# Score matmuls of two heads issued back to back in the neighbourhood attentions

## What is computed

```python
q = a @ w_q * 64 ** -0.5                     # 8 heads of 64, 256 rows
k, v = [ctx; a] @ w_k, [ctx; a] @ w_v        # 512 keys: 256 local, 256 context
s_loc = q k_loc^T + bias(rpb, window)        # -1e30 outside the window of 16 columns
s_ctx = q k_ctx^T
p = softmax([s_loc, s_ctx]);  y = p @ v
```

## Time and profile before

| | us |
|---|---|
| median of 3 runs (lowest, highest) | 3045.1 (3044.39, 3056.07) |
| the profiled execution: its time | 3047.46 |
| the profiled execution: its span | 3045.7 |
| PE busy in the span | 2736.5 (90%), 13754 matmul records |
| DVE busy | 788.7 (26%) |
| ACT busy | 453.7 (15%) |
| mean granted TensorE clock | 0.952 |
| "na0", from its first weight load to that of the low projection behind it | 1820.16 to 1864.61 |
| "na1", first weight load | 2482.05 |

### The profile page before, as it was taken

The page is one execution under the profiler, slowest core; times in us unless marked ns, Lnnn a source line. Parts: engine busy times, 40 slices in busy tenths (PEclk is TensorE's granted clock), DMA queues, the critical chain, the costliest instruction groups (busy, mean ns, idle before and its releaser), DMA issues.

```text
span 3045.7 us, 33992 instructions
## 1 busy us (share of the span) xinstructions
PE 2736.5 (90%) x13754; PEld 1856.9 (61%) x13754; DVE 788.7 (26%) x1893; ACT 453.7 (15%) x971; POOL 74.8 (2%) x144
## 2 busy tenths in 40 slices
PE   6998987889989969899999598898999897998998
PEld 2554544446567845555554356587788544687886
DVE  1344202221121261111111414414642224313002
ACT  2132002121120021000000113301000122301000
POOL 0000000000000000000000000000000000000000
PEclk9998998899999979999999799999999999999999
DMA  9874998999966519999999432143675211133330
GB/s 397 330 328 185 372 413 350 383 421 410 422 279 262 197 64 400 422 411 422 419 422 422 165 120 77 56 148 129 258 283 205 111 55 56 74 148 135 142 138 14
DMA packets 117580, 764.86 MB, mean 251 GB/s; under 512 B 12784, under 2 KB 15600, under 8 KB 34224
## 3 DMA queue, kind: packets, MB, share of 16 engines
q1 hardware_dynamic: 94352, 680.57, 55.3%
q0 software_dynamic: 20224, 74.26, 6.2%
q10 hardware_dynamic: 2848, 7.83, 0.6%
HBM read 759.20 MB, written 3.41 MB: 250 GB/s over the span
## 4 chain that ended last, share of the span: by engine, by line
PE 75%; DMA 14%; DVE 6%; issue 2%; ACT 2%; SPq 1%; POOL 0%; ACTq 0%; DVEq 0%
PE bank L542 73%; DMA ring<-in_stream 13%; PE bank L841 1%; PE bank L830 1%; SPq L422 1%; DMA work<-in_stream 1%; PE bank L546 1%; DVE work L1835 1%; DVE MX L1897 0%; ACT work L1432 0%; DVE work L1914 0%; DVE work L1694 0%; DVE work L1687 0%; DVE work L2349 0%; DVE X L2114 0%
## 5 line engine op out<-in xcount | busy, mean ns | idle before, releaser
L542 PE MATMUL bank<-A,ring 128*128 128x256 f32 (+1 forms) x3088 | 712.0, 390 | 17.7 <-issue 7.7
L542 PEld LDWEIGHTS bank<-A,ring 128*128 128x128 f32 x3088 | 588.8, 191 | 134.8 <-issue 43.7
L542 PE MATMUL bank<-ring,A 128*32 128x512 f32 (+3 forms) x2304 | 418.4, 638 | 82.3 <-DMA ring<-in_stream 71.4
L542 PE MATMUL bank<-work,ring 128*128 128x256 f32 x1696 | 386.5, 386 | 8.8 <-DVE work L1843 6.1
L542 PEld LDWEIGHTS bank<-work,ring 128*128 128x128 f32 x1696 | 326.0, 193 | 61.2 <-DVE work L1843 7.6
L542 PE MATMUL bank<-work 128*64 128x128 f32 (+5 forms) x2084 | 338.5, 332 | 14.9 <-DVE work L1772 5.2
L542 PEld LDWEIGHTS bank<-ring,A 128*32 128x32 f32 (+2 forms) x2304 | 127.9, 129 | 355.3 <-issue 228.1
L542 PE MATMUL bank<-A,work 128*128 128x256 f32 x1280 | 292.9, 386 | 20.0 <-ACT A L1330 11.4
L542 PEld LDWEIGHTS bank<-work 128*128 128x128 f32 (+2 forms) x2084 | 247.4, 172 | 79.2 <-issue 44.5
L542 PEld LDWEIGHTS bank<-A,work 128*128 128x128 f32 x1280 | 242.5, 192 | 79.5 <-issue 33.6
L542 PE MATMUL bank<-work,par_sb 128*128 128x256 f32 (+2 forms) x228 | 82.4, 500 | 75.7 <-ACT work L1432 23.0
(11 more groups left out here) (266 smaller groups left out, 1506.4 us busy)
## 6 DMA issues: line engine op xcount, KB each, us to landing
ring<-in_stream SPq DMA_DIRECT2D x648, 1024.0 KB, 12.6
work<-in_stream POOLq DMA_DIRECT2D x134, 512.0 KB, 8.7
X<-in_xt ACTq DMA_DIRECT2D x1, 2048.0 KB, 13.9
spill<-work ACTq DMA_DIRECT2D x3, 512.0 KB, 9.9
work<-spill POOLq DMA_DIRECT2D x3, 512.0 KB, 4.9
tab_sb<-in_tab_a ACTq DMA_DIRECT2D x1, 1120.0 KB, 18.6
X<-in_ctx2t ACTq DMA_DIRECT2D x1, 1024.0 KB, 15.5
out<-X SPq DMA_DIRECT2D x1, 1024.0 KB, 4.8
```

The costliest lines, as they stand in the source:

```text
L542: return pay(pe.matmul(o, w, x, start=start, stop=stop, tile_position=place), tells)
```

## The change

Three things change in `attention` and the table of banks:

- `SBANKS` names the banks for scores instead of counting them. The "na" calls get four (0, 1, 2 and 7), the "mla" calls keep 0 to 2 and "even" keeps 0 and 1. `score_bank` picks the bank of a unit; ACT and DVE read from it.
- In an "na" call PE makes scores in even steps alone, and for two units at once: scores of head h, scores of head h+1, then the bias of h, then the bias of h+1, each of the biases with its `at_s`. Odd steps have no scores. All else in the steps stays where it was: transposes of unit t-2 in every step, value matmuls in even ones. The "mla" and "even" calls go unit by unit as before.
- The wait for a free bank looks four units back for "na". For the first units of a call that isn't the first, PE waits for all exponentials of the calls before it.

```diff
-        SBANKS = {"even": 2, "na0": 3, "mla0": 3, "na1": 3, "mla1": 3}
+        SBANKS = {"even": (0, 1), "na0": (0, 1, 2, 7), "mla0": (0, 1, 2), "na1": (0, 1, 2, 7), "mla1": (0, 1, 2)}
+
+        def score_bank(name, g):
+
+            return bank[SBANKS[name][g % len(SBANKS[name])]]
@@
                 for t in range(nb * HEADS + 5):
-                    if t < nb * HEADS:
-                        g, b, h = u0 + t, t // HEADS, t % HEADS
-                        if g >= SBANKS[name]:
-                            pe.wait_ge(at_p, g - SBANKS[name] + 1)
-                        s = bank[g % SBANKS[name]]
-                        m = mm(s[:, :], q(h, b), k(h), True, bias is None, tells=bias is None)
+                    pair = 2 if name[:2] == "na" else 1
+                    if t < nb * HEADS and t % pair == 0:
+                        for i in range(t, t + pair):
+                            g, b, h = u0 + i, i // HEADS, i % HEADS
+                            if t >= len(SBANKS[name]):
+                                pe.wait_ge(at_p, g - len(SBANKS[name]) + 1)
+                            elif u0:
+                                pe.wait_ge(at_p, u0)
+                            m = mm(score_bank(name, g)[:, :], q(h, b), k(h), True, bias is None, tells=bias is None)
+                            if bias is None:
+                                m.then_inc(at_s, 1)
                         if bias is not None:
-                            m = pe.matmul(s[:, 0:T], ident, bias(h, b), start=False, stop=True)
-                        m.then_inc(at_s, 1)
+                            for i in range(t, t + pair):
+                                g, b, h = u0 + i, i // HEADS, i % HEADS
+                                pe.matmul(score_bank(name, g)[:, 0:T], ident, bias(h, b), start=False, stop=True)\
+                                  .then_inc(at_s, 1)
```

More of the change, by code:

```diff
@@ L1482, in attention @@
                             act.wait_ge(at_t, g - 2)
-                        act.activation(PR[:, g % 3, :], bank[g % SBANKS[name]][:, :], ACT.Exp, bias=NM[:, pb, h:h + 1],
+                        act.activation(PR[:, g % 3, :], score_bank(name, g)[:, :], ACT.Exp, bias=NM[:, pb, h:h + 1],
                                        scale=scale, accum_out=SM[:, pb, h:h + 1]).then_inc(at_p, 1)
@@ L1896, in attention @@
                         dve.wait_ge(at_s, g + 1)
-                        link(dve.reduce_max(MX[:, pb, h:h + 1], bank[g % SBANKS[name]][:, :], AXX))
+                        link(dve.reduce_max(MX[:, pb, h:h + 1], score_bank(name, g)[:, :], AXX))
                         if sink:
```

## The result

The changed kernel takes 3028.25 us (median of seven runs, 3023.43 to 3036.61), the kernel before 3047.45 (seven runs, 3044.39 to 3056.07): a ratio of 0.9938, 95% interval 0.992 to 0.9956, so 0.62% faster, between 0.44 and 0.80%. The medians are 19.2 us apart. That the level came out to 0.2 us is luck in part: with seven runs the median before is 2.35 us higher.

The account below looks back on a forecast made before the run. PE's own work was taken to bound the two na calls. Saving 8.5 us a call, 17.0 us in both, gave 3045.1 - 17.0 = 3028.1 us, range 3022 to 3041.

Parts of the forecast that it names:

- What bounds the call: In the two na calls, 2 x 44.45 us, PE's own work counts; PE is busy 42 of 44 us.
- Two scores side by side: Scores of two heads on PE, in different row halves, overlap fully: 0.86 + 0.01 us; 1.72 if not at all.
- The column halves: Value matmuls on PE, taken as nearest evidence: two weight loads under way within 20 ns, 16 records in 1.02 us.
- The staggered rival: Score records start strictly in order, so only two overlap: 3.4 us less saved per call, 3035 us; chance 0.06.
- Not side by side: Rival: a pair's scores don't overlap, only a shape change is saved: some 2 us a call, 3041; chance 0.08.
- Changes of shape: PE matmul shape changes per two heads fall from five to four; each costs about 0.2 us.
- The sum of a call: Start, five steady pairs and last pair of an na call together save 8.5 us, 17.0 in both calls.
- What could come late: DVE's scaling before the second transposes of a steady pair: ready at 3.33, wanted at 3.58, 0.25 us to spare.
- The DVE rival: DVE's chain 0.3 us late, second transposes wait 0.1 to 0.3 a pair: 3029 to 3032; chance 0.08 within 0.80.
- The clock: Rival: half clock granted in both na calls, a call becomes 70 us, 51 us slower in both, 3096; chance 0.03.
- Around the calls: Half-clock stretches behind the two na calls can fall differently by one or two, 2 to 4 us either way.
- The line at 0.5%: Whole time: 15.2 us can be told from no change, line at 3029.9; faster 0.57, same 0.39, slower 0.04.

Follow-up runs that it names:

- e1: The changed kernel with both heads' score operands taken from partitions 0 to 63: median 3039.42 us, against 3026.52 for the changed kernel on the same chip.
- e3: The changed kernel with order scores, bias, scores, bias, so a pair's scores are apart: 3057.92 us in one run, pair 5.41 us.
- e5: The changed kernel with a 512-column memset on DVE behind each maximum of na0 and na1: 3035.31 us in one run, pair 4.39 us.
- e4: The changed kernel with a 160-column memset on DVE behind each maximum of na0 and na1: 3039.17 us in one run, pair 4.17 us.
- e6: The changed kernel with the even head's bias added by DVE instead of PE: 3034.26 us, ratio 0.9938 to the kernel before the change.
- e2_bank_only: The changed kernel with four banks for scores but unit by unit as before, no pairing: 3050.01 us in one run, pair 5.26 us.
- e7_bias_late: The changed kernel with the even head's bias added by DVE from unit 4 on only: median 3028.29 us, ratio 0.9911 to the kernel before.

## Why the prediction was right

*What bounds the call.* Right: PE's own work, pair by pair, before and after.

*Two scores side by side.* Right, with the value taken, 0.86 + 0.01, and the 0.19 of a shape change behind it: scores to bias 1.06 us. The column halves were the right neighbours to read it from. The staggered rival would have shown 1.49 and is out: both records of the even head do not go ahead of the odd head's first. Whether the heads keep their order inside each pair of records the rows don't tell. "Not side by side" would have shown 1.91, which is what e1 shows when both heads lie in the same rows. Going from one half to the other costs 0.01 us at most (1.06 against a single head's 1.05).

*Changes of shape.* Right as far as shown: with four, five and six changes and nothing side by side the pair takes 5.02 (e1), 5.26 (before) and 5.41 us (e3), so 0.24 and 0.15 for one, where some 0.2 was forecast.

*The sum of a call.* Forecast and measured, in us:

| | forecast | measured |
|---|---|---|
| units 0 and 1 | 2.12 | 2.15 |
| units 2 and 3 | 4.23 | 4.11 |
| a steady pair | 4.16 | 4.17 |
| last pair with the emptying | 8.8 | 8.69 |
| a call | 35.9 | 35.79 |
| saved in both calls | 17.0 | 17.3 |

The terms listed for the last pair up to the transposes of unit 13 add up to 3.97, not to the 4.06 given; the 0.09 more are not named there. Without them the last pair would be 8.7, which is what it took.

*What could come late.* Right, to 0.01 us: 0.25 forecast, 0.26 by e5, and e4's 0.12 fits into it. The DVE rival didn't come: the second transposes have no wait for L1925 in the steady part.

*The clock.* The rival didn't come in the change: 1.00 in both calls. Half clock inside a call came in one run, e6, for a few us of "na1"; the waits before it are no sufficient reason, as shown there.

*Around the calls: right in its size, and luck in the sum.* The prediction let stretches of half clock behind the calls fall differently by one or two, 2 to 4 us either way. They did. Behind "na0" and behind "na1" the work is the same in all kernels here, yet it takes (us, from the weight loads' starts and the span's end):

| | the two calls | between them | behind "na1" | sum |
|---|---|---|---|---|
| before | 88.9 | 617.4 | 519.2 | 1225.5 |
| e2_bank_only | 88.9 | 617.5 | 519.2 | 1225.5 |
| e3_apart | 89.2 | 617.4 | 523.3 | 1229.9 |
| the change (each of three traces) | 71.6 | 615.9 | 521.0 | 1208.5 |
| e6_bias_dve | 69.4 | 617.4 | 521.5 | 1208.3 |
| e7_bias_late | 67.3 | 617.7 | 520.2 | 1205.2 |

The change gained 1.5 us between the calls and lost 1.9 behind "na1", so that only 0.3 of the 17.3 from the calls are given back. That these two nearly cancel is luck; e3 alone lost 4.1. The granted clock shows both. 20 us from 81 us behind the end of "na0", before and then after:

```profile
1945.60:1965.60 20.00, 17.48 (x98) 14.72 (x99) 5.65 (x15) 3.85 (x8) 0.00 (x0) 0.91 0.00 1
```

```profile
1934.70:1954.70 20.00, 17.01 (x103) 14.62 (x104) 6.05 (x18) 4.33 (x8) 0.00 (x0) 1.00 0.00 1
```

20 us from 24 us behind the end of "na1", before and then after:

```profile
2550.50:2570.50 20.00, 13.98 (x42) 9.60 (x43) 9.05 (x16) 5.60 (x13) 0.00 (x0) 0.74 0.28 105
```

```profile
2529.40:2549.40 20.00, 13.94 (x40) 9.90 (x41) 9.10 (x16) 4.85 (x12) 0.00 (x0) 0.66 0.28 105
```

From run to run of one kernel this does not vary: the sum was 1208.5 us in each of the three profiled executions of the change (first loads at 1817.92, 1824.07 and 1821.20 in spans of 3026.5, 3032.6 and 3029.7). What varies there lies in front of "na0", which nothing here touches: over all traces its first load stands at 1816.9 to 1828.4. So 17.0 us of the 19.2 between the medians belong to the change; the other 2.2 are no more than the spread in front of "na0".

*The chances.* The line at 0.5% was passed by the medians and, as nearly as said, by the stretch (17.0 us are 0.56%); the interval, from 0.44%, reaches below it.

## What to carry to other kernels

Here two fp32 matmuls of 512 columns with 64 contraction rows, one in partitions 0 to 63 and one in 64 to 127, into different banks, took the time of one (1.06 us to the next matmul) when nothing of another shape stood between them. One bias matmul between them took all of it back (5.41 us a pair against 4.17), and a change of shape cost some 0.2 us besides. Where such a pair is made at once, count the banks. Then work out the slack of the engine that reads them from the order of its steps, not from its busy share: DVE had over a microsecond of idle time in a pair and 0.26 us to spare. Where a part of a kernel repeats to a few hundredths of a us, compare that part from trace to trace: it shows a gain of 3 us that no median here could show. Take it apart once more, into what was changed and what follows, since what follows moved by up to 4 us without being touched.

## What the runs showed that was not expected

The half-clock stretches repeated from run to run of one kernel and changed from kernel to kernel. In e3_apart, with calls longer by 0.14 us each, the stretch from the first score load of "na0" to the end was 4.4 us longer than in e2_bank_only (1229.9 against 1225.5), though the calls account for 0.3 of it. The 25 us from 915 us behind the end of "na0", in e2 and then in e3, windows with the columns of the earlier trace rows:

```profile
2782.10:2807.10 25.00, 18.18 (x65) 13.29 (x64) 12.43 (x34) 9.43 (x19) 0.00 (x0) 0.86 0.23 85
```

```profile
2785.80:2810.80 25.00, 18.40 (x55) 13.03 (x54) 12.04 (x33) 9.43 (x19) 0.00 (x0) 0.73 0.23 85
```

The granted clock is 0.86 in the one and 0.73 in the other, at the same place of the work, and PE gets through fewer records in the second. This is one trace of each kernel. They differ in the order inside the calls as well as in the 0.14 us, so that the small shift is the cause is not shown; why the stretches fall as they do stays open.
